# RWKV chain: keys turned to token order by VectorE's block transpositions and an exchange through DRAM instead of identity products

## The reference

```python
def rwkv7_scan(r, w, k, v, kk, a, s0):
    # S_t = S (diag(w) - kk^T (a*kk)) + v^T k ; y_t = S_t r
    def step(s, inp):
        r_t, w_t, k_t, v_t, kk_t, a_t = inp
        s_kk = jnp.einsum('bhvk,bhk->bhv', s, kk_t)
        s = (s * w_t[:, :, None, :] - s_kk[..., None] * (kk_t * a_t)[:, :, None, :]
             + v_t[..., None] * k_t[:, :, None, :])
        return s, jnp.einsum('bhvk,bhk->bhv', s, r_t)
```

## Time and profile before

| | |
|---|---|
| median of 3 runs | 3620.71 us |
| lowest and highest | 3611.99, 3623.83 us |
| the profiled execution | 3625.17 us, its span 3623.4 us |
| mean granted TensorE clock | 0.985 |
| span of the chain, layer 0 | about 290 to 650 us |
| span of the chain, layer 3 | about 3000 to 3352 us |
| DMA issues of the chain: store of N (128 KB each) | 64, median 2.5 us to landing |
| load of its blocks, store of the inverse, load of it (64 KB each) | 32 each, 2.6, 1.9 and 2.2 us to landing |

### The profile page before, as it was taken

How to read it: one execution, slowest core, us unless ns; L and a number is a source line. 1 busy time by engine, 2 the same in 40 slices (tenths; PEclk the granted TensorE clock), 3 DMA queues, 4 the chain that set the end, 5 groups by cost and what they waited for, 6 DMA issues and landing times. The chain is left out here.

```text
span 3623.4 us, 74330 instructions
## 1 busy us (share of the span) xinstructions
PE 3453.8 (95%) x28645; PEld 2520.7 (70%) x28645; DVE 2500.4 (69%) x4570; ACT 1154.7 (32%) x2478; POOL 596.4 (16%) x1135
## 2 busy tenths in 40 slices
PE   7998998999999999999999999999999997888999
PEld 2447777588886455555888866678877546777887
DVE  7986665489897657563898955469986956664431
ACT  3034664223302444431233014323310235663210
POOL 2015553000000323320000000000000105552000
PEclk9998999999999999999999999999999999999999
DMA  6641111244453323223434520044434531111454
GB/s 204 210 144 21 23 24 32 71 128 126 126 163 96 100 83 102 79 78 99 128 124 127 163 81 27 27 125 130 126 119 127 180 118 25 24 24 27 133 152 134
DMA packets 584315, 365.07 MB, mean 101 GB/s; under 512 B 126144, under 2 KB 553480, under 8 KB 581928
## 3 DMA queue, kind: packets, MB, share of 16 engines
q1 hardware_dynamic: 557544, 250.40, 25.0%
q0 software_dynamic: 26432, 110.07, 8.7%
HBM read 348.73 MB, written 11.67 MB: 99 GB/s over the span
## 5 line engine op out<-in xcount | busy, mean ns | idle before, releaser
L274 PE MATMUL PS<-H,WR 128*128 128x512 f32 (+1 forms) x1424 | 477.1, 494 | 0.0
L567 DVE SCALAR_TENSOR_TENSOR WORK<-WORK,SC 128x512 f32<-128x512 f32 x616 | 418.4, 746 | 0.7
L274 PEld LDWEIGHTS PS<-H,WR 128*128 128x128 f32 x1424 | 267.9, 190 | 187.5 <-issue 167.2
L2525 PE MATMUL PS<-WORK 64*64 64x64 f32 (+2 forms) x6944 | 365.4, 233 | 27.6 <-ACT BIG L2822 17.3
L547 POOL DMA_DIRECT2D WORK<-in_ada_w_dram x88 | 66.2, 752 | 1831.0 <-DVE WORK L567 1013.9
L1450 PE MATMUL PS<-BIG,WR 128*128 128x512 f32 (+1 forms) x944 | 329.4, 503 | 4.8 <-DVE BIG L1074 1.5
L2525 PEld LDWEIGHTS PS<-WORK 64*64 64x64 f32 (+1 forms) x6944 | 286.2, 141 | 66.8 <-ACT WORK L2811 23.0
L1450 PEld LDWEIGHTS PS<-BIG,WR 128*128 128x128 f32 x944 | 175.7, 190 | 132.2 <-issue 112.0
L2811 ACT ACTIVATE WORK<-PS 128x64 f32<-128x64 f32 (+3 forms) x528 | 161.5, 325 | 300.4 <-PE PS L2525 295.6
L988 ACT ACTIVATE WORK<-PS 128x512 f32<-128x512 f32 x252 | 135.1, 541 | 346.7 <-PE PS L921 314.4
L921 PE MATMUL PS<-BIG 128*128 128x256 f32 x984 | 223.9, 380 | 0.0
(11 more groups left out here) (362 smaller groups left out, 6420.6 us busy)
## 6 DMA issues: line engine op xcount, KB each, us to landing
WORK<-in_ada_w_dram POOLq DMA_DIRECT2D x88, 1024.0 KB, 6.2
WR<-in_ffn_w_in_dram SPq DMA_DIRECT2D x220, 256.0 KB, 2.9
BIG<-in_ffn_w_in_dram SPq DMA_DIRECT2D x132, 256.0 KB, 3.4
WR<-in_ffn_w_out_dram SPq DMA_DIRECT2D x106, 256.0 KB, 2.8
WR<-in_ssd_w_in_dram SPq DMA_DIRECT2D x96, 256.0 KB, 2.8
BIG<-scratch_dram POOLq DMA_DIRECT2D x8, 2048.0 KB, 8.0
BIG<-in_ffn_w_out_dram SPq DMA_DIRECT2D x36, 256.0 KB, 3.1
BIG<-in_ada_w_dram SPq DMA_DIRECT2D x4, 2048.0 KB, 18.8
```

What stands on the lines that cost most here:

```text
L274: mm = pe.matmul(outs, WR[:, slot, k, 0:m], rhs(k), start=first and k == 0, stop=last and k == nk - 1)
L567: lag(vec.scalar_tensor_tensor(ACC3[:, s_], w, by, ACC3[:, s_], ALU.mult, ALU.add), label)
L2525: return pe.matmul(o, lhs, rhs, start=start, stop=stop)
```

## The change

TensorE's and ScalarE's part of "HB" is dropped. In its place VectorE makes four transpositions "TB" for each tile and segment, one for each direction d and each of n = 0 (`ADS`) and n = 1 (`SD`). They turn 32x32 blocks within each 32 partitions, so half of the blocks then lie on the wrong 32 partitions; these go out to DRAM by four DMAs and come back by four (32 partitions, 4 runs of 512 bytes on each, 64 KB per DMA). `BK` has a new layout, in which the 64 columns of a chunk lie 4 elements apart; "S" takes them so as its stationary operand. The new steps stand at k = 6, 8, 10, 12 in slots (i, 0) and at k = 0, 1, 3, 9 in slots (i, 1), all late. In SyncE's queue the exchange of (i, 0) stands between `blocks_in(i, 1)` and `inverse_out(i, 1)`, and that of (i, 1) between `blocks_in(i + 1, 0)` and `inverse_out(i + 1, 0)`.

```diff
-        G2, BK, G1R = by_chunk(P), by_chunk(P), by_chunk(Q)
+        G2, G1R = by_chunk(P), by_chunk(Q)
+        BK = work(2 * NQ * P).rearrange("p (s d n a f) -> p s d n a f", s=2, d=2, n=2, a=2)
@@ slot_steps, s == 0
-                          (12, "HB", both[0], 0, 0), (15, "HB", both[0], 0, 1), (16, "H2", both[1], 0),
-                          (18, "HB", both[1], 0, 0), (20, "HB", both[1], 0, 1)]
+                          (16, "H2", both[1], 0)]
+                late += [(k, "TB", i, 0, d, n) for k, (d, n) in zip((6, 8, 10, 12), ((0, 1), (1, 1), (0, 0), (1, 0)))]
@@ slot_steps, s == 1
-                          (3, "HB", both[0], 1, 0), (4, "HB", both[0], 1, 1), (7, "H2", both[1], 1),
-                          (10, "HB", both[1], 1, 0), (11, "HB", both[1], 1, 1)]
+                          (7, "H2", both[1], 1)]
+                late += [(k, "TB", i, 1, d, n) for k, (d, n) in zip((0, 1, 3, 9), ((0, 1), (1, 1), (0, 0), (1, 0)))]
@@ rwkv_sp
+            swap = swapped.rearrange("(s b p d n f) -> s b p d n f", s=2, b=4, p=32, d=2, n=2)
+            def swap_out(i, s_):
+                sp.wait_ge(vec_done, C.at(f"{t}.t{i}.tb{s_}"))
+                if i:
+                    sp.wait_ge(swap_loaded, C.at(f"{t}.t{i - 1}.bk{s_}"))
+                for b in range(4):
+                    sp.dma_start(swap[s_, b ^ 1], BK[32 * b:32 * b + 32, s_, :, :, 1 - b % 2, :]).then_inc(
+                        swap_stored, C.mark(swap_stored, f"{t}.t{i}.swap{s_}" if b == 3 else None, 16))
+            def swap_in(i, s_):
+                sp.wait_ge(swap_stored, C.at(f"{t}.t{i}.swap{s_}"))
+                for b in range(4):
+                    sp.dma_start(BK[32 * b:32 * b + 32, s_, :, :, 1 - b % 2, :], swap[s_, b]).then_inc(
+                        swap_loaded, C.mark(swap_loaded, f"{t}.t{i}.bk{s_}" if b == 3 else None, 16))
             for i in range(KD):
                 grams_out(i, 0)
                 blocks_in(i, 0)
                 if i == 0:
                     grams_out(i, 1)
                     blocks_in(i, 1)
+                else:
+                    swap_out(i - 1, 1)
+                    swap_in(i - 1, 1)
                 inverse_out(i, 0)
                 inverse_in(i, 0)
                 if i:
                     grams_out(i, 1)
                     blocks_in(i, 1)
+                swap_out(i, 0)
+                swap_in(i, 0)
                 inverse_out(i, 1)
                 inverse_in(i, 1)
+            swap_out(KD - 1, 1)
+            swap_in(KD - 1, 1)
@@ rwkv_pe: by_token is dropped; vt waits for t{n}.a1 alone; chain_s
-                    pe.wait_ge(act_done, C.at(f"{t}.{q}.bk{c // 4}"))
+                    pe.wait_ge(swap_loaded, C.at(f"{t}.t{i}.bk{c // 4}"))
+                by_token = [BK[:, c // 4, d, n].rearrange("p a (f c) -> p (a f) c", c=4)[:, :, ch % 4] for n in range(2)]
...
-                        mm(PS[hs, d, P:P + Q], BK[hs, d, c, Q:P], v_tok[hs, tok(ch)], stop=False)
+                        mm(PS[hs, d, P:P + Q], by_token[1][hs], v_tok[hs, tok(ch)], stop=False)
...
-                        last = mm(PS[hs, d, P:P + Q], BK[hs, d, c, 0:Q], US[d][hs, :], start=False)
+                        last = mm(PS[hs, d, P:P + Q], by_token[0][hs], US[d][hs, :], start=False)
@@ rwkv_act: by_token is dropped; replacement
-                    act.wait_ge(pe_done, C.at(f"{t}.{2 * n - 2 + d}.hb1"))
+                    act.wait_ge(pe_done, C.at(f"{t}.{2 * n - 2 + d}.h21"))
+                    act.wait_ge(vec_done, C.at(f"{t}.{2 * n - 2 + d}.turned1"))
@@ rwkv_vec
+            def by_token(i, s_, d, n):
+                half, q = SEGS[s_], 2 * i + d
+                vec_last()
+                if i:
+                    vec.wait_ge(pe_done, C.at(f"{t}.{q - 2}.sp{min(4 * s_ + 3, NQ - 2)}"))
+                src = (SD if n else ADS[i % 2])[:, d, half].rearrange("p (c b t) -> p b c t", b=2, t=32)
+                dst = BK[:, s_, d, n].rearrange("p a (f c) -> p a c f", c=4)
+                lag(vec.transpose(dst, src), f"{t}.{q}.turned{s_}" if n else f"{t}.t{i}.tb{s_}" if d else None)
```

More of the change, by code:

```diff
@@ L190, in program @@
         gram_stored = sem("gram_stored")
+        swap_stored = sem("swap_stored")
+        swap_loaded = sem("swap_loaded")
         blocks_loaded = sem("blocks_loaded")
@@ L2465, in rwkv_sp @@
             parts_sp(f"mo{l}", a["rw_wo"][j], [(m, 0) for m in range(2)])
-            wide, narrow = blocks_dram
+            wide, narrow, swapped = blocks_dram
             def grams_out(i, s_):
@@ L2538, in vt @@
             def vt(n):
-                pe.wait_ge(act_done, C.at(f"{t}.{2 * n - 1}.bk1") if n else C.at(f"{t}.t{n}.a1"))
+                pe.wait_ge(act_done, C.at(f"{t}.t{n}.a1"))
                 for ch in range(NQ):
@@ L2609, in grams_k @@
                 done(last, f"{q}.h2{s}")
[L2611 to L2630, removed]
             def z_step(q, s, m):
@@ L2792, in rwkv_pe @@
             pe.wait_ge(act_done, C.at(f"{t}.ve{KD - 1}"))
-            run({**staging, "GT": grams, "R": grams_r, "H2": grams_k, "HB": by_token, "Z": z_step, "X": x_step, "W": chain_w, "U": chain_u, "S": chain_s, "P2": post2, "P3": post3,
+            run({**staging, "GT": grams, "R": grams_r, "H2": grams_k, "Z": z_step, "X": x_step, "W": chain_w, "U": chain_u, "S": chain_s, "P2": post2, "P3": post3,
                  "O": output})
@@ L2884, in first_grams @@
                         grams(n, s_, d)
[L2886 to L2890, removed]
             def z_step(q, s_, m):
@@ L2946, in rwkv_act @@
                         stage_first(staging, u)
-            run({**staging, "GT": grams, "HB": by_token, "Z": z_step, "W": chain_w, "S": chain_s, "YE": y_end,
+            run({**staging, "GT": grams, "Z": z_step, "W": chain_w, "S": chain_s, "YE": y_end,
                  "P1": post1, "P2": post2, "P2e": post2e})
@@ L3209, in rwkv_vec @@
             run({**staging,
-                 "IB0": first_inverse, "E": expand, "Rv": grams_r, "H2": grams_k, "X": x_step, "U": chain_u, "S": chain_s, "P2v": post2, "P3": post3})
+                 "TB": by_token, "IB0": first_inverse, "E": expand, "Rv": grams_r, "H2": grams_k, "X": x_step, "U": chain_u, "S": chain_s, "P2v": post2, "P3": post3})
             vec_last()
@@ L3358, in build @@
         blocks_dram = [nc.dram_tensor(f"blocks{n}_dram", (size,), F32, kind="Internal").ap()
-                       for n, size in enumerate((16 * BLOCK_STRIDE, P * BLK * BLK))]
+                       for n, size in enumerate((16 * BLOCK_STRIDE, P * BLK * BLK, 2 * P * T))]
         counts = program(nc, args, out, draft, scratch, blocks_dram, **OPTIONS)
```

## The result

The changed kernel takes 3737.89 us in the median of 4 runs (3735.47 to 3742.83), beside 3620.59 for the kernel before (3611.99 to 3623.83): a ratio of 1.0334, with an interval of 1.0317 to 1.0351. It is slower by 117 us, where +52 was forecast and the range ended at 3712. Its profiled execution has a span of 3734.9 us at a mean granted clock of 0.970 (0.985 before). All executions in this document are in the fast state except one of run 15, which took 9357.99 us for no known reason and does not move that run's median of 11.

The account below looks back on a forecast made before the run. TensorE looked like the bound, with SyncE's inverse exchange, nearly without slack, as a second bound. The terms 63 - 12 - 8.4 + 4.2 + 5.6 = +52 us gave 3673 us, with an 8 in 10 range of 3606 to 3712.

Parts of the forecast that it names:

- the pitch of 16 bytes at nothing: S's 224 state updates: weight loads with columns 16 bytes apart, put at nothing in the sum.
- TensorE's relief: Dropped identity products, 59 us: 0.6 us counted per slot (i, 1), nothing in slots (i, 0); -8.4 us.
- The queue term, +63: SyncE, slots (i, 0): inverse's store waits for transpositions and exchange, 7.25 us less slack, over 14 slots: +63 us.
- The push of VectorE: Slots (i, 0): three earlier transpositions push VectorE back, 0.8 us (0 to 2.0), part of the 7.25.
- What is late next, -12: Behind a late expansion TensorE is ahead, so the time from expansion to U's copy shrinks: -12 us in all.
- the clock, +5.6: Long TensorE waits lower the granted clock: 0.4 us per slot, +5.6 us (0 to 24).
- The rival: S's strided weight loads cost: +30 us on the sum, 3703 us; chance 0.13.
- its sign: Strided loads would show by slots (i, 1) growing too, or S's records lying more than 0.03 us apart.
- Transpositions, +4.2: VectorE, slots (i, 1): two of four transpositions free, the other two cost 0.3 us a slot: +4.2 us.

Follow-up runs that it names:

- run 15: Changed kernel without the exchange's transfers, with packed columns, S reading zeros, and the identity products back on TensorE, unused: 3625.59 us.
- run 3: Kernel before without the identity products and their evictions, S taking zeros as keys: 3630.83 us.
- run 16: Kernel before with the identity products kept on TensorE, only their evictions and use dropped, S taking zeros as keys: 3620.95 us.
- run 9: Changed kernel without the exchange's transfers and with packed columns, S taking packed zeros as keys: 3631.76 us.
- run 7: Changed kernel without the exchange's stores and loads, S taking zeros of the same 4-element pitch as keys: 3659.38 us.
- run 5: Changed kernel with each chunk's 64 columns packed side by side, the exchange in runs of 128 bytes: 3727.5 us.
- run 13: Changed kernel, transpositions late as they are, with pairs of chunks interleaved, columns 8 bytes apart: 3724.07 us.
- run 14: Changed kernel with the identity products put back on TensorE, unused and not evicted: 3739.77 us.
- run 2: Kernel before with ScalarE evicting the keys 4 elements (16 bytes) apart and S loading them so: 3637.61 us.
- run 12: Kernel before with both the exchange's transfers in SyncE's queue and the columns of BK 4 elements apart: 3688.61 us.
- run 6: Changed kernel with packed columns and all transpositions early (k = 1 to 4 in slots (i, 0); 0, 1, 3, 4 in slots (i, 1)): 3644.34 us.
- run 11: Changed kernel with early transpositions and pairs of chunks interleaved, columns 8 bytes apart: 3641.94 us.
- run 1: Kernel before with only the exchange's eight DMAs per segment and their waits added to SyncE's queue, on an unused region: 3655.82 us.

## Why the prediction was right and wrong

Three steps of the prediction failed. It put the pitch of 16 bytes at nothing, where it cost 27 us; it put TensorE's relief at -8.4, where the runs show none or a loss of up to 10; and it sized the exchange at 57 us, where it cost 78. The first two are wrong in kind, the third in size.

By subtraction the 117 us fall apart in this order: products dropped +10 (3630.8 less 3621.0, runs 3 and 16), transpositions +1 (3631.8, run 9), pitch +27 (3659.4, run 7), exchange +78 (3737.9). In another order the shares differ: with the exchange in place, the pitch is worth 10 to 14 (runs 5, 13), and the exchange 96 (3727.5 less 3631.8), and the dropped products nothing (run 14). The medians are of different rounds, so each share can be off by some 3 us. Both orders say that the exchange is the main part.

**The queue term, +63: right in kind, too small.** In slot (4, 0) it went from L3102's end at 500.72 thus: 0.77 to the first store (forecast 0.55), 4.26 to the first load (3.9), 2.85 to the inverse's store (2.0). The push of VectorE before it was 1.06 (15.33 from expansion to L3102's end, against 14.27; forecast 0.8). That is 8.94 against 7.25, in all four pieces over my value. Three lie inside my bounds, and the fourth, the issues of the loads, lies over its bound of 2.7. The issue of a DMA with 512-byte runs was undervalued most: 0.6 to 0.7 us each with the gap, where I took 0.5 from the lower half of the earlier trace rows. Over all 14 slots the inverse was stored 84 us later (309.4 less 225.6), where the sum had 63: this is where most of the 21 us of the exchange were missed. By the difference of run 7 and the changed kernel, slots (i, 0) lost 79 us.

**What is late next, -12, and the clock, +5.6.** The shift came: expansion to copy takes 2.14 us (515.56 less 513.42), less than 3.1. Slots (i, 1) did not get shorter by it, most likely because of the clock. It was priced from one dip at 0.61 over 5 us, at 0.4 a slot; here TensorE had run out of work during the wait of 7.17 us, and the next 5 us of work went at 0.50. Slot (4, 1) has a mean of 0.87 where it had 1.00, and the 12 slots (i, 1) one of 0.842, against 0.966 in run 7. By run 7 and the changed kernel the exchange costs slots (i, 1) 3 us in sum, where I had -6.4.

**The 16-byte pitch at nothing: the step that failed outright.** I let the sum go by the reading under which a pitch of 4 float32 is free, and gave the other 0.13. The rival's mechanism showed: S's loads got slower, slots (i, 1) grew, which the prediction had named as its sign, and by runs 7 and 9 the pitch costs +27, near its +30. That nearness is in part luck. The 27 hold the transpositions' stores too (128 times 0.2 us of VectorE's time), which the rival did not count, and no run has the pitch in the loads alone: run 2 has it in ScalarE's evictions as well. How the 27 divide stays open. On the Trainium skill (SBUF — State Buffer, "Door 1: The DMA port swizzle"): what it says of consecutive accesses within a line of 16 bytes, that two or more of them give full bandwidth, agrees with every row here; its list, by which 4 float32 is how far one can stride for free, does not. With columns 2 elements apart two fall in a line, and that was free (140 ns, 446 ns); 4 apart each has a line of its own, and that was not (171 ns, 647 ns). The doubtful case sat right at the line, and the other half of the same note decided against it: that should have been more than 13 in 100.

**TensorE's relief, -8.4: wrong sign.** It was worth nothing in the changed kernel (run 14) and less than nothing where waits are short (runs 3, 15). I had written that it would be lost in slots (i, 0); I didn't see that in slots (i, 1) less work before the wait can mean a longer wait and a lower clock behind it. That the clock is the link is supported by the mean clock of slots (i, 1), 0.915 in run 3 and 0.981 in run 16, 0.955 in run 9 and 0.989 in run 15, but no run held the clock apart from the work.

**Transpositions, +4.2 and the push.** With a packed store they cost 1 to 3 us in all, no more than noise. The strided store took 647 ns, within 445 to 890 and over the value that I took; what that costs in time is part of the 27.

**The total.** The terms also work on each other (run 12, +16 beyond the sum), which a sum of separate terms cannot show. With 78 for the exchange in place of 56.6 (63 - 12 + 5.6), 27 for 0, 10 for -8.4 and 1 for 4.2, the +52 becomes the +117 measured. (It must: the four are differences of successive runs.) 21, 27, 18 and -3 are the four errors in this order of subtraction, and all but the last lie on one side; by run 14 the error of the relief is 8 and not 18, and the exchange's is larger. The range was too narrow because it took the bounds of the terms as if they would offset each other.

Nothing beats the kernel before. Even with the exchange free and the columns packed (run 9) the change takes 3632 us, so with the transpositions where they stand there, no place for the exchange in the queue could make it pay; early transpositions without transfers were not run.

## What to carry to other kernels

When a queue serves an exchange that has no slack, new transfers must not stand between a result and its store; count their issues and landings from the last instruction that they wait for, and then ask for the order that lets them run while the result is being made. Taking work off the busiest engine gained nothing here, where a transfer of fixed latency ends the slot: the engine then idled, and its clock was lower behind the wait. A layout that saves a copy is read many times, so price its pitch where it is read (here 8 loads in each of 224 updates) and where it is stored, and when two readings of a rule differ at exactly that pitch, take the cautious one.

## What the runs showed of the hardware

- Pitch of float32 columns in SBUF: 4 or 8 bytes, transpositions of 128x256 in 446 or 447 ns and weight loads of 138 to 144 ns in the mean of the group of 1920 (runs 5, 6, 9, 11, 13); 16 bytes, 647 ns (the changed kernel) and 167 to 171 ns (the changed kernel, runs 2 and 7).
- ScalarE's evictions of 128x512 from PSUM: 593 ns in the mean of 72 with packed stores, 1043 ns when 64 of the 72 store 16 bytes apart (the kernel before, run 2).
- SyncE's issue of 64 KB on 32 partitions took 418 ns with one run of 2 KB a partition, 594 with four of 512 bytes, 603 with runs of 256 and 622 with runs of 128 bytes (medians of run 1, the changed kernel, runs 13 and 5).
- 59 us of TensorE's work removed made a kernel 10 us slower, and put back unused 6 us faster in another (runs 3, 16, 9, 15); in the changed kernel they made no difference (run 14).
- A wait of 7.17 us on TensorE was followed by 5 us at a granted clock of 0.50 (the changed kernel).
